# First stages of a hybrid transformer layer on one core: order of the input rows, low weight parts on GpSimd, token half 0 first, small parameters later

## What is computed

```
h   = rmsnorm(x, g_mix_pre)                 # 1024 tokens x 1024
z   = h @ w_in                              # q, k, v, u, qx, gates
mkv = rmsnorm(mem, g_mem) @ w_mem_kv        # 256 memory tokens; km = keys, vm = values
y_mem  = softmax(qx @ km / sqrt(128)) @ vm  # cross-attention, 4 heads
y_attn = windowed attention on q, k, v with rotary positions and sinks
y_ssm  = diagonal state-space layer on u, then GELU and a gated projection
x = x + rmsnorm((sum of gated branches) @ w_out, g_mix_post)
x = x + rmsnorm(square(relu(rmsnorm(x) @ w_up)) @ w_down, g_mlp_post)
```

## Time and profile before

| | us |
|---|---|
| median of 3 runs | 1585.14 |
| lowest, highest run | 1581.22, 1585.4 |
| the profiled execution | 1585.63 |
| its span | 1583.8 |
| PE busy | 1547.2 (98%) |
| DVE busy | 833.4 (53%) |
| ACT busy | 460.8 (29%) |
| POOL busy | 119.6 (8%) |
| chain that ended last: PE, DVE, DMA | 94%, 3%, 2% |

### The profile page before, as it was taken

The page is one execution under the profiler, slowest core; times in us unless marked ns, Lnnn a source line. Parts: engine busy times, 40 slices in busy tenths (PEclk is TensorE's granted clock), DMA queues, the critical chain, the costliest instruction groups (busy, mean ns, idle before and its releaser), DMA issues.

```text
span 1583.8 us, 18390 instructions
## 1 busy us (share of the span) xinstructions
PE 1547.2 (98%) x7403; PEld 1297.1 (82%) x7403; DVE 833.4 (53%) x1581; ACT 460.8 (29%) x647; POOL 119.6 (8%) x190
## 2 busy tenths in 40 slices
PE   6899999999999999999999999999999999999997
PEld 5788779878888888888888888888888888888886
DVE  6838658657746725446766643333333333333348
ACT  5443744332222234221343322112130212121132
POOL 2000010041220221100000200000000000000000
PEclk9899999999999999999999999999999999999999
DMA  8301120242112245324432420111101111101104
GB/s 298 88 27 53 41 92 29 87 127 93 67 54 100 60 138 184 131 83 156 145 109 80 146 74 33 54 53 53 53 26 53 53 53 53 51 28 53 53 1 173
DMA packets 82208, 130.94 MB, mean 83 GB/s; under 512 B 13120, under 2 KB 55136, under 8 KB 82144
## 3 DMA queue, kind: packets, MB, share of 16 engines
q1 hardware_dynamic: 66400, 76.03, 14.7%
q0 software_dynamic: 15744, 54.03, 9.9%
HBM read 104.88 MB, written 25.17 MB: 82 GB/s over the span
## 4 chain that ended last, share of the span: by engine, by line
PE 94%; DVE 3%; DMA 2%; issue 1%; ACT 1%; SPq 0%; POOL 0%; DVEq 0%; ACTq 0%
PE bank L1426 87%; PE bank L1439 2%; DMA raw<-in_w_mem_kv_dram 1%; PE bank L1644 1%; PE bank L1531 1%; PE bank L1658 1%; PE bank L1599 1%; PE bank L1627 0%; PE bank L1546 0%; PE bank L1662 0%; DVE wlo L305 0%; DMA tok<-in_x_dram 0%; DVE prob L1000 0%; DVE mx L998 0%; DVE hTlo L933 0%
## 5 line engine op out<-in xcount | busy, mean ns | idle before, releaser
L1426 PE MATMUL bank<-hThi,whi 128*128 128x512 f32 x1184 | 463.7, 392 | 1.2 <-DVE hTlo L933 0.7
L1426 PE MATMUL bank<-hThi,wlo 128*128 128x512 f32 x1184 | 461.7, 390 | 0.0
L1426 PE MATMUL bank<-hTlo,whi 128*128 128x512 f32 x1184 | 461.7, 390 | 0.0
L1426 PEld LDWEIGHTS bank<-hThi,whi 128*128 128x128 f32 x1184 | 222.9, 188 | 48.4 <-issue 2.7
L1426 PEld LDWEIGHTS bank<-hThi,wlo 128*128 128x128 f32 x1184 | 222.8, 188 | 46.7
L1426 PEld LDWEIGHTS bank<-hTlo,whi 128*128 128x128 f32 x1184 | 222.9, 188 | 45.8
L299 ACT ACTIVATE whi<-raw 128x2048 fp32r<-128x2048 f32 x65 | 124.1, 1911 | 377.7 <-PE bank L1426 333.2
L1426 PE MATMUL bank<-whi,yhi 128*128 128x512 f32 x512 | 199.3, 389 | 0.8 <-DVE wlo L305 0.8
L1426 PE MATMUL bank<-whi,ylo 128*128 128x512 f32 x512 | 199.2, 389 | 0.0
L1426 PE MATMUL bank<-wlo,yhi 128*128 128x512 f32 x512 | 199.2, 389 | 0.0
L305 DVE TENSOR_TENSOR wlo<-raw,whi 128x2048 fp32r<-128x2048 f32 x65 | 148.8, 2290 | 70.2 <-ACT whi L299 69.5
(11 more groups left out here) (314 smaller groups left out, 1854.9 us busy)
## 6 DMA issues: line engine op xcount, KB each, us to landing
raw<-in_w_in_dram SPq DMA_DIRECT2D x34, 512.0 KB, 4.6
raw<-in_w_up_dram SPq DMA_DIRECT2D x32, 512.0 KB, 4.3
raw<-in_w_down_dram SPq DMA_DIRECT2D x32, 512.0 KB, 4.3
gate_scratch<-scr POOLq DMA_DIRECT2D x48, 256.0 KB, 2.3
tok<-gate_scratch POOLq DMA_DIRECT2D x24, 512.0 KB, 3.6
raw<-in_w_mem_kv_dram SPq DMA_DIRECT2D x8, 512.0 KB, 8.7
y_scratch<-yst POOLq DMA_DIRECT2D x16, 256.0 KB, 2.5
yst<-y_scratch POOLq DMA_DIRECT2D x16, 256.0 KB, 4.3
```

Of the source, the lines that this page charges most:

```text
L1426: ins = T.matmul(dst, lhs(k)[p], rhs(k)[q], start=start and k == 0 and i == 0, stop=stop and k == kt - 1 and i == 2)
```

## The change

1. POOL asks for tile 4 only when unit 1 has landed and for tile 6 only when unit 2 has landed, so tiles 6 to 9 are requested behind unit 2.
2. The low parts of units 2 to 5 are made by POOL (`split_low`) and no longer by DVE; POOL requests positions, inv_freq and sinks behind the low part of unit 2. Before the low part of unit 6, DVE waits until `w_lo` has come to 6, so that the counts rise in order.
3. The 16 matmuls hi*hi of unit 0 stand ahead of PE's wait for the low parts; the other 32 follow.
4. The first half of `qx` (unit 4) multiplies token half 0 (tiles 2 to 5) for both column blocks first, then half 1, each behind a wait for its own tiles; `spar` stands behind those four banks instead of ahead of them, on PE and on ACT.

```diff
-STAGES = [("front", 28), ("spar", 1), ("qx", 8), ("xsc", 16), ...
+STAGES = [("front", 28), ("qx", 8), ("spar", 1), ("xsc", 16), ...
# POOL
+            def split_low(u):
+                pool.wait_ge(w_hi, u + 1)
+                pool.wait_ge(w_lo, u)
+                hi, lo = parts(u)
+                g.tensor_tensor(lo, raw[:, u % 2, :], hi.bitcast(f32), sub).then_inc(w_lo, 1)
             pool.wait_ge(w_loaded[0], 32)
             for idx in range(2, 10):
+                if idx in (4, 6):
+                    u = idx // 2 - 1
+                    pool.wait_ge(w_loaded[u % 2], 32 * (u // 2 + 1))
                 if idx >= 7:
                     pool.wait_ge(h_made, idx - 6)
                 g.dma_start(xtile(idx), ...)
...
+            split_low(2)
             g.dma_start(yst2 ..., a["positions"] ...)
...
+            for u in range(3, U_QX + 2):
+                split_low(u)
# ACT
-            n = FIRST["spar"]
-            copy_out(n, spar ..., banks[n % 8][:, 0:48])
             for s in range(2):
...
-                for i in range(2):
-                    for half in range(2):
-                        copy_out(n0 + 2 * i + half, tokq[:, 2 * s + i, half * 512:half * 512 + 512])
+                for m in range(4):
+                    i, half = (m // 2, m % 2) if s else (m % 2, m // 2)
+                    copy_out(n0 + m, tokq[:, 2 * s + i, half * 512:half * 512 + 512])
                 if s == 0:
+                    n = FIRST["spar"]
+                    copy_out(n, spar ..., banks[n % 8][:, 0:48])
                     act.wait_ge(trig_arg, 1)
# DVE
                 norm_lo(3 + 2 * s)
-                prep_lo(dve, s + 2)
...
+            dve.wait_ge(w_lo, U_QX + 2)
             prep_lo(dve, U_QX + 2)
# PE
+            pe.wait_ge(w_hi, 1)
+            pe.wait_ge(split_hi, 4)
+            for i in range(2):
+                for k in range(KT):
+                    T.matmul(banks[...][:, 0:256], hi[:, k, i * P:i * P + P], mThi[:, k, :], start=k == 0, stop=False)
+            unit(0)
             for idx in range(2):
                 for e in range(2):
                     wait_taken(pe, norm_event(idx, e))
...
+            unit(U_QX)
+            for hf in range(2):
+                for idx in range(2 + 4 * hf, 6 + 4 * hf):
+                    for e in range(2):
+                        wait_taken(pe, norm_event(idx, e))
+                for i in range(2):
+                    n = FIRST["qx"] + 2 * hf + i
+                    wait_free(pe, n)
+                    product(banks[n % 8][:, :], ..., hT(half(hf)), KT).then_inc(bank_full[n % 8], 1)
             pe.wait_ge(s5_dt, 1)
             n = FIRST["spar"]
...
-            for s in range(2):
-                project(U_QX + s, FIRST["qx"] + 4 * s)
+            project(U_QX + 1, FIRST["qx"] + 4)
```

More of the change, by code:

```diff
@@ L42 @@
 U_GATE = [9, 12, 13] + list(range(14, 23))
-STAGES = [("front", 28), ("spar", 1), ("qx", 8), ("xsc", 16), ("q", 8), ("kv", 4), ("xpv", 24), ("ssc0", 8), ("g0", 4), ("vwin", 4),
+STAGES = [("front", 28), ("qx", 8), ("spar", 1), ("xsc", 16), ("q", 8), ("kv", 4), ("xpv", 24), ("ssc0", 8), ("g0", 4), ("vwin", 4),
           ("ssc1", 8), ("u", 8), ("g1", 4), ("spv", 24), ("g2", 4), ("spc", 2), ("s5a0", 6), ("g3", 4),
@@ L586, in _ @@
                          ACT.Copy).then_inc(s5_dt, 1)
-            n = FIRST["spar"]
-            copy_out(n, spar[:, :, :].rearrange("p a b -> p (a b)"), banks[n % 8][:, 0:48])
             for s in range(2):
@@ L593, in _ @@
                     prep_hi(act, U_QX + s + 1, n0 - 1)
-                for i in range(2):
-                    for half in range(2):
-                        copy_out(n0 + 2 * i + half, tokq[:, 2 * s + i, half * 512:half * 512 + 512])
+                for m in range(4):
+                    i, half = (m // 2, m % 2) if s else (m % 2, m // 2)
+                    copy_out(n0 + m, tokq[:, 2 * s + i, half * 512:half * 512 + 512])
                 if s == 0:
+                    n = FIRST["spar"]
+                    copy_out(n, spar[:, :, :].rearrange("p a b -> p (a b)"), banks[n % 8][:, 0:48])
                     act.wait_ge(trig_arg, 1)
@@ L1453, in _ @@
             norm_transposes(1)
+            hi, lo = wviews(0, KT)
+            pe.wait_ge(w_hi, 1)
+            pe.wait_ge(split_hi, 4)
+            for i in range(2):
+                for k in range(KT):
+                    T.matmul(banks[(FIRST["front"] + 4 + i) % 8][:, 0:256], hi[:, k, i * P:i * P + P], mThi[:, k, :], start=k == 0, stop=False)
+            unit(0)
             for idx in range(2):
@@ L1456, in _ @@
                     wait_taken(pe, norm_event(idx, e))
-            for s in range(4):
+            for i in range(2):
+                n = FIRST["front"] + 4 + i
+                for k in range(KT):
+                    T.matmul(banks[n % 8][:, 0:256], hi[:, k, i * P:i * P + P], mTlo[:, k, :], start=False, stop=False)
+                    ins = T.matmul(banks[n % 8][:, 0:256], lo[:, k, i * P:i * P + P], mThi[:, k, :], start=False, stop=k == KT - 1)
+                ins.then_inc(bank_full[n % 8], 1)
+            norm_transposes(2)
+            norm_transposes(3)
+            for s in range(1, 4):
                 n0 = FIRST["front"] + 4 + 6 * s
@@ L1483, in project @@
                         .then_inc(bank_full[n % 8], 1)
+            unit(U_QX)
+            w = [v.rearrange("p k (i c) -> p k i c", i=2) for v in wviews(U_QX, KT)]
+            for hf in range(2):
+                for idx in range(2 + 4 * hf, 6 + 4 * hf):
+                    for e in range(2):
+                        wait_taken(pe, norm_event(idx, e))
+                for i in range(2):
+                    n = FIRST["qx"] + 2 * hf + i
+                    wait_free(pe, n)
+                    product(banks[n % 8][:, :], lambda k: (w[0][:, k, i], w[1][:, k, i]), hT(half(hf)), KT).then_inc(bank_full[n % 8], 1)
             pe.wait_ge(s5_dt, 1)
@@ L1491, in _ @@
             ins.then_inc(bank_full[n % 8], 1)
-            for idx in range(2, 10):
-                for e in range(2):
-                    wait_taken(pe, norm_event(idx, e))
-            for s in range(2):
-                project(U_QX + s, FIRST["qx"] + 4 * s)
+            project(U_QX + 1, FIRST["qx"] + 4)
             tokq = tok[:, :].rearrange("p (i t) -> p i t", i=4)
```

## The result

Over 20 runs each, timed side by side, the changed kernel takes 1587.2 us and the kernel before 1582.81 us in the median, 4.4 us less. The measured ratio is 1.0019, 95% interval 1.001 to 1.0027, which is some 3 us; it is not the quotient of the two medians, which would be 1.0028. The forecast was 1.4 us less than before; it became 3 to 4 us more. Two things in the single times matter for all that follows. The kernel before is usually faster than the execution whose profile stands ahead of the prediction (1585.63 us): of its 76 times in this and the later comparisons 10 are 1585 us or more. The profile after is of an execution of 1582.03 us, one of the lower group.

The account below looks back on a forecast made before the run. PE's end of qx, delayed by front-stage waits, was taken as the bound, DVE as a second. POOL's holds start qx at 60.9 to 62.2 us, ending 0.8 to 2.1 us earlier: 1584.2 us, range 1580.5 to 1588.0 us (8 in 10: 1573 to 1589.5).

Parts of the forecast that it names:

- the 2.8 us of low clock fall away there: At qx: with no pause in front of it, the 2.8 us that half clock cost it are won.
- 1585.63 - 1.4: Total: the profiled execution's 1585.63 us less the middle gain of 1.4 us gives 1584.2 us.
- POOL's unit 4 misses tile 7's norm_h: Front stage: that row, free at 46.7 us against POOL's 46.2, escapes the hold; 1582.0 us, kept within the forecast case.
- norm_h of tile 7 meets POOL's unit 4: Front stage: POOL's unit 4, 46.2 to 51.1 us, holds tile 7's row, which then runs 51.1 to 52.3 us.
- another rival's condition: If norm_lo is held too (0.11), POOL's unit 5, 59.9 to 64.8 us, holds norm_h of tile 9 to 66.0 us.
- the term: Reordered requests: six transfers of 1.3 us from about 26 us bring unit 3 at 34 us, not 39.06 us.
- the price on POOL: Low parts on POOL: each 128x2048 instruction takes 4.9 us, bounds 4.0 and 5.0 us.
- DVE stands still: Front stage: rstd2's tiny instructions and norm_h wait until POOL's instruction ends; tile 4's norm_h moves from 28.65 to 33.6 us.
- norm_lo is free: DVE's norm_lo, reading one operand from PSUM, is taken not to be held beside POOL.
- the rival that gave 1590.6 us: Front stage: POOL holds norm_lo too, qx begins at 67.5 us and ends 5.0 us later; chance 0.11.
- side by side: Front stage: POOL costs DVE little, qx begins at 51.3 us, 11.6 us earlier, 1574.0 us; chance 0.24.
- What is won is at qx: Its first half needs neither spar (2.6 us) nor tiles 8 and 9 (0.7 us), and 2.8 us of low clock go.

Follow-up runs that it names:

- the lower group: Unaltered changed kernel: 8 of its first 20 times, from 1580.34 to 1583.81 us.
- the second comparison: The changed kernel timed again, unaltered, against the kernel before: 1584.4 us over 11 runs, ratio 1.0016.
- e17: The kernel before, unaltered, profiled in another execution: 1581.22 us.
- e18: The kernel before, unaltered, profiled a further time: 1581.07 us.
- order A: Profiled executions of the unaltered changed kernel in which POOL holds neither tile 7's nor tile 9's row: 1580.79 to 1582.56 us.
- order B: Four profiled executions of the unaltered changed kernel in which tile 7's row is held beside POOL's unit 4: 1583.7 to 1584.51 us.
- Order C: The one profiled execution of the unaltered changed kernel in which POOL's unit 5 starts first and tile 9's row is held: 1587.91 us.
- e10: The changed kernel, unaltered, profiled in another execution, with tile 7's row held: 1583.7 us.
- the upper group: Unaltered changed kernel: 12 of its first 20 times, from 1586.5 to 1588.85 us.

## Why the prediction was wrong, step by step

Two steps failed. One is the base: "the 2.8 us of low clock fall away there" and "1585.63 - 1.4". The other is the order of POOL and DVE, where "POOL's unit 4 misses tile 7's norm_h" was kept "inside my case". The price of a hold and what it holds were right.

**The base.** 1585.63 us is 2.8 us above the 1582.81 us of the kernel before. The forecast time of the changed kernel, 1584.2 us, is 3.0 us under the 1587.2 us measured; that part is the order, below. In the second comparison (1584.4 against 1582.09 us) the forecast time is right to 0.2 us and the base is the whole miss. The sum's end of qx, 106.8 us, came from an execution in which product 3 took 7.53 us and the clock was at half for 6.8 us around the start of qx. In e17 and e18 product 3 is at full clock and the half clock at qx lasts 3.4 us. There qx takes 45.4 us; at full clock it takes 43.8 us (21.79 + 22.00 in the profile after), so 1.6 us can be won at it and not 2.8. The forecast named both stretches in its own rows and counted their recovery as a gain of the change; the run of 1581.22 us was already in its table. Against e17 and e18 (xsc at 104.8 us) order A is 0.3 us ahead (104.54), B 2.3 us behind (107.10), C 6.2 us behind (110.96). e17 and e18 are themselves 1 to 1.7 us faster than the medians of the kernel before, and no trace shows an execution at the median.

**The order: right for one of three.** The steps of the sum describe order B: tile 4's row 33.6 us (33.15 in e10), tile 5's 36.0 (35.55), POOL's unit 4 from 46.2 (46.01), the meeting with tile 7's row, which ends at 52.3 (51.6), product 3 partly at a low clock, qx from 60.9 to 62.2 us (61.66 to 61.94 in the four), total 1584.2 us (1583.7 to 1584.51). The step that failed is "norm_h of tile 7 meets POOL's unit 4", which the sum takes as certain on a margin of 0.5 us (row free at 46.7, POOL at 46.2). Its miss was named, priced at 1582.0 us (A: 1580.79 to 1582.56) and kept inside the case. But with that miss product 3 starts sooner, unit 5 is split sooner, and POOL's unit 5 meets tile 9's row (56.7 to 58.2 us for both in A and C). That question was asked only under another rival's condition, and there it costs the most: 12 of the 20 runs are in the upper group. Order C, 1587.91 us, was inside the range by luck, since the range had not been drawn for it.

**Part 1: right in kind, small in effect.** Unit 2 was split at 24.19 us (24.5 forecast), unit 3 at 36.31 us and not 34: the term was 2.3 us too short. From about 26 us on the six transfers took 10.3 us, 1.7 us each and not 1.3. Alone the part gains 1.6 us.

**Part 2, the price on POOL:** 4.9 us forecast, 4.62 and 4.61 us measured where it started first, 5.03 and 5.49 us where a row of DVE was ahead of it. **DVE stands still:** right, the tiny instructions of rstd2 included (4.62 and 4.46 us). **norm_lo is free:** right (1.28 us for two at 48.13 us beside POOL), so the rival that gave 1590.6 us did not happen; nor did side by side. (In that rival's sum 67.5 and 43.8 us make 111.3 and not 111.8 us.) On norm_lo the Trainium skill, page "SBUF — State Buffer", section "Who interferes with whom", had stated that a DVE instruction with at most one SBUF operand outside the fast modes is not held; the traces agree, with that number. It also states that two SBUF operands contend only with a POOL instruction that reads, and that tensor_scalar can contend through its fast mode; the 2.28 us and the 1.80 us beside memsets agree with both halves.

**Part 4:** "What is won is at qx" was right: 4.0 us alone, with the waits for spar gone and qx at full clock. That the 16 early matmuls save nothing was not tried by itself.

**What was missing**, too, was the comparison of the parts with one another. The sum shows rstd2 moving from 28.65 to 33.6 us and does not ask what the kernel would be without part 2. That kernel is 1576.46 us: the other parts gain 5.6 us, and part 2 takes 5.9 us even when its rows always win (1582.34 us), 8 us as it is (1584.4 us, measured side by side with them).

## What to carry to other kernels

Work moved from DVE to POOL can cost DVE up to the full length of each POOL instruction where a DVE instruction with two SBUF operands or a TENSOR_SCALAR comes to stand beside it, however small (4.5 us here for 2.28 us saved), so ask first what the chain of DVE would be without the move. Where two engines come to such a resource within a microsecond of one another, price both orders at every meeting and fix the order with a semaphore (here that alone turned 1584.4 into 1582.34 us). Profile several executions of the kernel before too: a profile with an uncommon stretch of low clock can make a change look like its cure.

## What the runs showed of the hardware

- A write-only POOL instruction (memset 128x2048, three in 5.54 us) holds a DVE TENSOR_SCALAR of 128x2 for 1.80 us and leaves a TENSOR_TENSOR with two SBUF operands at its 2.28 us. One theory had it free altogether.
- The same subtraction of 128x2048 takes POOL 4.5 to 4.6 us when it starts first and 5.03 to 5.53 us when a DVE row is under way, which is 4.5 us and what the row had left (0.56 us at 47.65 us, 1.03 us at 57.41 us).
- Differences of 0.2 to 0.9 us at 46 and 57 us give the same program three orders, with times of 1580.8 to 1582.6, 1583.7 to 1584.5 and 1587.9 us, while the 1460 us behind differ by 1 us.
- With a product at half clock another of two engines came first (not set by an experiment): with the low clock absent, for 3.4 us, or for 6.8 us around product 2, the qx of the same kernel began at 61.8, 59.4 and 64.9 us.
